# mLSTM head loop of a two-block kernel: a second buffer for the backward scores, and another order of work on four engines

## The reference

```python
def mlstm_scan(q, k, v, ig, log_fg):      # per chunk, with running maximum m_t
    log_d = cum[..., :, None] - cum[..., None, :] + igc[..., None, :]
    d_mat = jnp.exp(jnp.where(tril, log_d, -jnp.inf) - m_t[..., None])
    scores = jnp.einsum('bhtd,bhsd->bhts', qc, kc) * d_mat
    num = jnp.einsum('bhts,bhse->bhte', scores, vc) + ...
    den = jnp.sum(scores, axis=-1) + ...
    h_out = num / jnp.maximum(jnp.abs(den), jnp.exp(-m_t))[..., None]

h_m = (mlstm_scan(q_m, k_m, v_m, ig_fwd, lfg_fwd)
       + flip_seq(mlstm_scan(flip_seq(q_m), flip_seq(k_m), ...)))
mlstm_out = head_rmsnorm(from_heads(h_m), mlstm_g, MLSTM_HEADS) * jax.nn.sigmoid(m_o)
return jnp.concatenate([hgrn_out, mlstm_out], axis=-1) @ w_out
```

## Time and profile before

| | us |
|---|---|
| median of 3 runs | 1682.1 |
| lowest and highest | 1680.78, 1685.4 |
| the profiled execution | 1681.14 |
| its span in the trace | 1679.3 |
| mLSTM loop in it, from the first g to the first out2 product | 1047.61 to 1104.73 |

### The profile page before, as it was taken

How to read it: one execution, slowest core, us unless ns; L and a number is a source line. 1 busy time by engine, 2 the same in 40 slices (tenths; PEclk the granted TensorE clock), 3 DMA queues, 4 the chain that set the end, 5 groups by cost and what they waited for, 6 DMA issues and landing times.

```text
span 1679.3 us, 18987 instructions
## 1 busy us (share of the span) xinstructions
PE 1616.4 (96%) x7258; PEld 1270.9 (76%) x7258; DVE 981.5 (58%) x1412; ACT 686.3 (41%) x1066; POOL 148.4 (9%) x153
## 2 busy tenths in 40 slices
PE   5999999999999999999999999789999999999997
PEld 1588765677888888887888787578877888888885
DVE  6986687775644334546788596655434553535352
ACT  4521465324443123335554578836433322212131
POOL 0221000252000000013000000332000100000001
PEclk9999999999999999999999999899999999999999
DMA  9544114422232233223232021235111322222221
GB/s 312 191 150 141 60 52 151 151 101 93 60 100 88 93 121 100 81 76 119 98 135 92 26 70 57 94 117 209 50 51 51 113 88 101 100 100 100 100 100 50
DMA packets 112600, 173.89 MB, mean 104 GB/s; under 512 B 3851, under 2 KB 56651, under 8 KB 112012
## 3 DMA queue, kind: packets, MB, share of 16 engines
q1 hardware_dynamic: 108220, 158.05, 27.8%
q0 software_dynamic: 4304, 14.81, 2.7%
HBM read 168.53 MB, written 4.33 MB: 103 GB/s over the span
## 4 chain that ended last, share of the span: by engine, by line
PE 83%; DVE 9%; DMA 3%; ACT 2%; issue 2%; SPq 1%; DVEq 0%; ACTq 0%
PE bank L896 17%; PE bank L898 17%; PE bank L897 17%; PE bank L933 6%; PE bank L934 6%; PE bank L938 5%; DMA weight_slots<-in_w_mod 2%; PE bank L1206 2%; PE bank L1126 1%; PE bank L1138 1%; PE bank L1444 1%; PE bank L1336 1%; DVE weight_slots_lo L2377 1%; PE bank L1401 1%; PE bank L1426 1%
## 5 line engine op out<-in xcount | busy, mean ns | idle before, releaser
L3260 POOL TENSOR_TENSOR arena<-arena 128x512 f32<-128x512 f32 (+1 forms) x56 | 76.7, 1377 | 970.7 <-ACT arena L1651 966.9
L898 PE MATMUL bank<-hx_hi,weight_slots_lo 128*128 128x512 f32 x320 | 124.7, 390 | 0.0
L3215 DVE TENSOR_TENSOR weight_slots_lo<-weight_slots,weights_hi 128x2048 fp32r<-128x2048 f32 x30 | 67.4, 2289 | 95.5 <-ACT weights_hi L2336 95.5
L2336 ACT ACTIVATE weights_hi<-weight_slots 128x2048 fp32r<-128x2048 f32 x30 | 55.8, 1909 | 161.1 <-DMA weight_slots<-in_w_up 115.5
L1620 ACT ACTIVATE weights_hi<-weight_slots 128x2048 fp32r<-128x2048 f32 (+2 forms) x46 | 77.3, 1723 | 90.1 <-DMA weight_slots<-in_ffn_w_down 57.6
L897 PE MATMUL bank<-xn_lo,weights_hi 128*128 128x512 f32 x288 | 112.1, 389 | 0.0
L896 PE MATMUL bank<-sq_hi,weights_hi 128*128 128x512 f32 x256 | 99.6, 389 | 0.0
L897 PE MATMUL bank<-sq_lo,weights_hi 128*128 128x512 f32 x256 | 99.6, 389 | 0.0
L898 PE MATMUL bank<-sq_hi,weight_slots_lo 128*128 128x512 f32 x256 | 99.6, 389 | 0.0
L1606 ACT ACTIVATE arena<-bank 128x512 f32<-128x512 f32 (+2 forms) x99 | 49.1, 532 | 94.2 <-PE bank L898 45.6
L2377 DVE TENSOR_TENSOR weight_slots_lo<-weight_slots,weights_hi 128x2048 fp32r<-128x2048 f32 (+2 forms) x35 | 68.1, 1981 | 27.0 <-ACT weights_hi L1620 27.0
(11 more groups left out here) (459 smaller groups left out, 4077.6 us busy)
## 6 DMA issues: line engine op xcount, KB each, us to landing
weight_slots<-in_w_in SPq DMA_DIRECT2D x24, 1024.0 KB, 7.5
weight_slots<-in_ffn_w_up SPq DMA_DIRECT2D x22, 1024.0 KB, 6.4
weight_slots<-in_w_up SPq DMA_DIRECT2D x16, 1024.0 KB, 6.8
weight_slots<-in_w_down SPq DMA_DIRECT2D x16, 1024.0 KB, 6.8
weight_slots<-in_w_mod SPq DMA_DIRECT2D x14, 1024.0 KB, 10.3
arena<-in_w_mod POOLq DMA_DIRECT2D x32, 256.0 KB, 3.3
weight_slots<-in_w_out SPq DMA_DIRECT2D x8, 1024.0 KB, 7.8
weight_slots<-in_w_xkv SPq DMA_DIRECT2D x8, 1024.0 KB, 7.5
```

The source lines that it names most:

```text
L898: return mm(ps, ll, rh, start=False, stop=stop)
L2336: A(W_hi[:, s % 2, a:b], W[:, s % 2, a:b], ACT.Copy).then_inc(w_hi, 1)
L3215: V.tensor_tensor(W_lo[:, s % 2, a:b], W[:, s % 2, a:b], W_hi[:, s % 2, a:b].bitcast(F32), ALU.subtract).then_inc(w_lo, 1)
L3260: G.tensor_tensor(acc, acc, sq[i % 2][:, 0:width], ALU.add).then_inc(sq_added, 1)
```

## The change

All of it lies in and around the loop over the four heads.

- **Buffers.** The score tiles were one set for each direction (`S2`). Now the forward scores have one set, and the backward scores have two, used by even and odd heads. The new one is at tiles 66 to 69. `head_scores` of the backward direction waits for num_b of two heads before, no longer for that of the head before. Because the region of tiles 66 to 69 is written again by a later load of x, SP now also waits for num_2_b_1 before that load.
- **DVE.** The forward and the backward scores of head h + 1 run behind each other in cycle h. Before, the backward ones ran at the start of cycle h + 1. `head_scaled(h - 1)` comes behind them, `lstm_out(h - 1)` behind `directions_added(h)`. The split of half 1 of the out2 weights moves from cycle 3 to the end of cycle 2. The low parts of the hgrn tiles and of heads 0 to 2 move behind the loop.
- **ACT.** The decays of head 1, both directions, come directly before the loop. In cycle h both decays of head h + 2 run. Before, cycle h held the backward decay of h + 1 and the forward one of h + 2. The output gates with their two table loads move from ahead of the loop to cycle 1. The high parts of the hgrn tiles and of heads 0 and 1 move to the end of cycle 2. Both halves of the out2 weights are split in cycle 2 ahead of `head_factor(2)`.
- **PE.** The transposes of head h - 1 come behind num backward of head h, no longer ahead of it.

The number of instructions and their shapes stay as they are.

The core of the diff:

```diff
--- before.py
+++ after.py
@@ jobs
+        if h >= 0:
+            j += [f"num_{h}_b_{p}" for p in range(2)]
         if h >= 1:
             j += [f"ht_{h - 1}"]
-        if h >= 0:
-            j += [f"num_{h}_b_{p}" for p in range(2)]
@@ buffers
-        S2 = [tiles(32, 4), tiles(36, 4)]
+        S2_f, S2_b = tiles(32, 4), [tiles(66, 4), tiles(36, 4)]
+
+        def S2(h, d):
+
+            return S2_b[h % 2] if d else S2_f
@@ SP
+            done(sp, f"num_{HEADS - 2}_b_1")
             load(xb, x_rest, "x_back")
@@ PE (and S2(h, d) in state_output)
+                if h >= 0:
+                    state_output(h, 1)
                 if h >= 1:
                     head_transposed(h - 1)
-                if h >= 0:
-                    state_output(h, 1)
@@ ACT
             decay(1, 0, "f")
+            decay(1, 1, "b")
+
+            def output_gates():
+
+                for m in range(HC):
+                    evicted(act, f"mo_{m}")
+                    A(mix2[:, 4 + m, :], mix2[:, 4 + m, :], ACT.Sigmoid).then_inc(sem("gate_ready"), 1)
+                log_exp_tables()
...
             for h in range(HEADS):
                 forward_scaled(h)
-                if h + 1 < HEADS:
-                    decay(h + 1, 1, "b")
-                if h == 0:
+                if h == 1:
+                    output_gates()
+                if h + 2 < HEADS:
+                    decay(h + 2, 0, "f")
+                    decay(h + 2, 1, "b")
+                elif h + 2 == HEADS:
+                    split_w("out2", 0)
+                head_factor(h)
+                if h + 2 == HEADS:
                     act.wait_ge(sem("ho_gated"), HEADS)
                     for k in range(HC):
                         split_x(mix2_hi[:, k, :], mix2[:, k, :])
-                else:
-                    lstm_high(h - 1)
-                if h + 2 < HEADS:
-                    decay(h + 2, 0, "f")
-                elif h + 2 == HEADS:
-                    split_w("out2", 0, (0,))
-                head_factor(h)
-                if h + 2 == HEADS:
-                    split_w("out2", 0, (1,))
+                    lstm_high(0)
+                    lstm_high(1)
+            lstm_high(2)
             split_w("out2", 1)
             lstm_high(HEADS - 1)
@@ DVE
-                if h:
-                    done(dve, f"num_{h - 1}_{c}_1")
+                if h > d:
+                    done(dve, f"num_{h - 1 - d}_{c}_1")
...
-            head_scores(0, 0, "f")
+            for d, c in enumerate("fb"):
+                head_scores(0, d, c)
+            head_normed(3)
+            head_gated(3)
             for h in range(HEADS):
-                head_scores(h, 1, "b")
-                if h == 0:
-                    head_normed(3)
-                    head_gated(3)
-                else:
+                forward_limits(h)
+                if h + 1 < HEADS:
+                    for d, c in enumerate("fb"):
+                        head_scores(h + 1, d, c)
+                if h:
                     head_scaled(h - 1)
-                forward_limits(h)
-                if h + 1 == HEADS:
-                    split_w("out2", 0, (1,))
+                directions_added(h)
                 if h:
                     lstm_out(h - 1)
-                if h + 1 < HEADS:
-                    head_scores(h + 1, 0, "f")
-                directions_added(h)
-                if h == 0:
-                    for k in range(HC):
-                        split_x("mix2", k, mix2_lo[:, k, :], mix2[:, k, :], mix2_hi[:, k, :])
-                else:
-                    lstm_low(h - 1)
+                if h + 2 == HEADS:
+                    split_w("out2", 0, (1,))
+            for k in range(HC):
+                split_x("mix2", k, mix2_lo[:, k, :], mix2[:, k, :], mix2_hi[:, k, :])
+            for h in range(HEADS - 1):
+                lstm_low(h)
             head_scaled(HEADS - 1)
```

More of the change, by code:

```diff
@@ L1425, in state_output @@
                                 evicted(pe, f"g_{h}_{j}")
-                            ins = mm(out_, S2[d][:, j, P * i:P * i + P], Vm[:, j, h, :], start=j == sources[0], stop=j == sources[-1])
+                            ins = mm(out_, S2(h, d)[:, j, P * i:P * i + P], Vm[:, j, h, :], start=j == sources[0], stop=j == sources[-1])
                     end(ins)
@@ L2218, in _ @@
             norm_factor("norm_ho_3", features=P)
-            for m in range(HC):
-                evicted(act, f"mo_{m}")
-                A(mix2[:, 4 + m, :], mix2[:, 4 + m, :], ACT.Sigmoid).then_inc(sem("gate_ready"), 1)
-            log_exp_tables()
             decay(1, 0, "f")
+            decay(1, 1, "b")
[4 more added lines that the diff above has]
+                log_exp_tables()
             def lstm_high(h):
@@ L3037, in head_scores @@
                     g = full(dve, f"g_{h}_{j}")
[L3038 removed]
+                    ins = V.scalar_tensor_tensor(S2(h, d)[:, j, lo:hi], g[:, lo:hi], float(P) ** -0.5, mD(h, c)[n][:, lo:hi],
                                                  ALU.mult, ALU.mult)
```

1 line of the change is left out of this document (removed).

## The result

| us | before | changed |
|---|---|---|
| median (4 runs each on one chip) | 1682.77 | 1668.62 |
| lowest and highest | 1680.78, 1685.40 | 1666.98, 1669.01 |
| the profiled execution, and its span | 1681.14, 1679.3 | 1666.98, 1665.2 |
| loop: first g to first out2 product | 1047.61 to 1104.73 = 57.12 | 1047.07 to 1090.65 = 43.58 |
| first to fifth out2 product | 22.35 | 22.36 |

The ratio of the times is 0.9914, 95% interval 0.9901 to 0.9926. 14.15 us are gone from the median. In the profiled execution 13.54 of them are gone from the loop. The profiled execution of the changed kernel is the fastest of its four; its median lies 1.64 us above it. Behind T0 nothing was given back.

The account below looks back on a forecast made before the run. PE, busy 96%, could regain only waits (17.7 us for DVE's scores) and low-clock time; afterwards ACT's queue is longest. Loop gain 13.0 less 1.0 for clock gives 12.0: 1681.14 to 1669.1, plus 0.96 for median 1670.1; range 1665.5 to 1676.

Parts of the forecast that it names:

- T0: Start of the first out2 product, where the loop ends: 1104.73 before, forecast 1091.7, a gain of 13.0 us.
- the clock cost: Out2 starting at PE's lower clock after two waits: 0 to 2.0 us, taken as 1.0 against the gain.
- ACT's queue: ACT from 1051.7 to its first weight half: decays, scalings, gates, factors, half sum to 30.6 us without gaps, ending 1082.3.
- POOL and DVE block each other: Out2 weight halves: DVE's, ready near 1084.2, waits for POOL's until 1086.9, then takes 2.27, ending 1089.1.
- the banks: At out2's start: banks of num forward of head 3 were claimed not to be among the first four; no size given.
- no blocking: Rival: POOL and DVE weight halves do not block; head 3's forward scaling sets T0 near 1090.2; 1668.6, chance 0.08.
- the second set of tiles: Backward score tiles: with both directions in one run, a second set can take away PE's 17.7 us of waits.
- the change does not do what it says: Rival: PE waited for ACT, not the single buffer; moving the gates alone gives all; forecast's time, no separate chance.
- Table loads at twice their row: Rival: the gates' two loads on ACT each take 1.3 us more, 2.6 in all; 1672.7, chance 0.05.
- Handoffs of 0.15 us: Rival: some twenty ACT and DVE links take 0.15 us more each, T0 3 to 4 later; 1674, chance 0.11.
- rivals of the low clock: PE at 1.2 GHz through the loop (no gain, 1681) or on through out2 (slower, 1691.4); chance 0.04 each.
- the slower rival: Low clock stays through out2: the 22.35 us behind T0 take 44.7; 1691.4, chance 0.04.

Follow-up runs that it names:

- e11: Changed kernel with the four hgrn splits back in cycle 0 on ACT and DVE; median 1672.06, loop 45.70 us.
- e12: Changed kernel with two more ACT table loads among the output gates in cycle 1, same numbers computed; median 1674.24, loop 46.31 us.
- e6: Changed kernel with DVE's out2 weight half moved to cycle 3, behind the scaling of head 2; median 1668.94, loop 42.76 us.
- e10: e8 with ACT's first weight half moved to cycle 1 and most hgrn splits behind forward scaling of head 3; median 1672.15, loop 45.25 us.
- e9: Changed kernel with the decays back in the cycles they had before the change; median 1682.49, loop 56.00 us.
- e1: Changed kernel with one set of backward score tiles instead of two; median 1669.27, loop 43.59 us.
- e3: Changed kernel with the output gates ahead of the loop and one set of backward score tiles; median 1675.83, loop 47.51 us.
- e2: Changed kernel with the output gates and their table loads ahead of the loop again; median 1670.00, loop 42.80 us.
- e7: Changed kernel with the transposes of the previous head ahead of num backward again; median 1672.82, loop 47.03 us.
- e8: Changed kernel with both edits of e2 and e6: gates ahead of the loop, DVE's weight half later; median 1670.32, loop 41.57 us.
- e5: Kernel before the change with only the output gates moved to cycle 1; median 1680.89, loop 56.07 us.

## Why the prediction held, step by step

The forecast was 1670.1 and the median came to 1668.62; a profiled 1669.1 stood against 1666.98. Of these 2.1 us, 0.54 lies ahead of the loop, 1.0 is the clock cost, and 0.5 is in the loop. That the median is nearer, by 1.5 us, is luck: the forecast put it 0.96 above the profiled execution, and it lay 1.64 above. Times below are compared after taking 0.54 off the forecast's.

| step | forecast | minus 0.54 | trace |
|---|---|---|---|
| first decay | 1051.7 | 1051.2 | 1051.23 |
| ACT's first half done, POOL half begins | 1082.4 | 1081.9 | 1082.00 |
| POOL half ends | 1086.9 | 1086.4 | 1086.53 |
| DVE half ends | 1089.1 | 1088.6 | 1088.68 |
| head 2 scaled | 1090.8 | 1090.3 | 1090.18 |
| T0 | 1091.7 | 1091.2 | 1090.65 |

- **ACT's queue** was the right model. The sum of 30.6 us from rows of before was good to 0.3 us, and the claim of no gaps held. e11 and e12 confirm it from outside: 2.14 us of splits gave 2.12, 2.71 us of loads gave 2.73.
- **POOL and DVE block each other:** the forecast had 4.9 us for the DVE half, the trace 4.94. e6 shows 2.28 without POOL beside it. "SBUF — State Buffer" of the Trainium skill, "SBUF: two separate sides", calls the port pair that the two engines share an exclusive lock, held for the whole instruction by whichever starts first; among DVE's instructions it names those with two inputs in SBUF. The traces agree, with 4.94 here, 4.47 in e10, where POOL was 0.62 us ahead, and 0.74 for the instruction that reads a bank. In e9 `head_scaled(1)` began 0.82 us ahead of POOL's half, behind POOL's transfer issue, and was held all the same.
- **The end of the loop:** 0.9 us were set aside for the transposes and handoffs. They took 0.47 (1090.18 to 1090.65). This is the 0.5 us within the loop.
- **The clock cost** of 1.0 was mis-sized. The step allowed for the two waits before T0 to leave PE at the low clock when out2 begins, and took the middle. They did not: the granted clock was back at 1.00 at 1086 us, and the wait of 2.56 behind it did not lower it. From T0 to the fifth product it was 22.36 us, against 22.35. The range taken, 0 to 2.0, was nearly right all the same: e1, e3, e12 paid 1.6, e2 paid 1.1, e7 0.5, and e8 2.5. The reason given for the middle, that both waits are shorter than the 5.5 and 7.1 behind which the level was low, misses a row that it had: behind the wait of 4.16, shorter than 4.9, the 14 records take 2.45, 0.18 each, and the granted clock in the kernel before was 0.50 from 1083 to 1085.
- **PE's waits:** forecast 4.9, 3.5 and little else, 9 in all. Measured 4.87, 2.56 and 0.41, 7.8 in all. The second is shorter because head 3's products ended at 1087.67, where the forecast less 0.54 has 1086.9; they ran longer at the low clock than it had.
- **A wrong step: the banks.** The prediction said that the banks of num forward of head 3 are not among the first four of out2. They are. In e6 and e8 the first out2 product waits 1.49 and 2.02 us for ACT L2204. In the changed kernel that scaling ended at 1090.40, 0.25 us before T0, so the mistake cost nothing. One of the prediction's rivals, no blocking, had this dependence right, with a T0 1.5 us earlier; e6, which takes the blocking away, gained 0.8.
- **A wrong attribution: the second set of tiles.** The prediction gave the 17.7 us of waits to the second set and the one run of both directions together. e1 shows the same loop without the set. The gain belongs to the order: both directions' scores in one run need the decays a cycle sooner (e9: without them, nothing is gained), late hgrn splits (5.4 us alone in the old order, 2.1 in the new), and late transposes (3.45). The second set and the gates' place stand in for each other (e1, e2, e3). No run puts the scores of the two directions apart again with all else as changed, so the share of that edit alone is not shown. That before the change PE waited for the bank and not for the tile, as the prediction itself said, fits e1; with the gates first one set is not enough (e3).
- **The rivals.** Moving the gates alone gives 1 us of loop (e5), so "the change does not do what it says" falls. Table loads at twice their row fall with e12. Handoffs of 0.15 us fall with the table above. Both rivals of the low clock asked for it through the loop or through out2; in the changed kernel it holds for one stretch, which begins during the wait ahead of the transposes at 1080.30 and is over by 1086. The price of the slower rival rested on the 22.35 us behind T0, where the worst that a run showed was 2.5 more (e8).
- **The load of x and the low parts behind the loop** cost nothing: from the fifth product to the end of the span it is 552.2 us in both kernels.

**No version beat the changed kernel in the median.** e6 and e8 shorten the loop by 0.8 and 2.0 us. Their medians are 1668.94 and 1670.32, with intervals that overlap. The profiled executions show where the gains went. That of e6 begins its loop 0.77 us later than that of the changed kernel and takes 1.8 more behind the fifth out2 product. That of e8 begins 1.64 later and takes 2.5 more to the fifth product and 1.7 behind it. One of the four executions of e8 took 1666.53, at a mean granted clock of 0.995 (the other three 1670.12 to 1670.89, at 0.991 and 0.992). That is below all four of the changed kernel, but it was not profiled.

## What to carry to other kernels

When one buffer makes an engine wait, add up the whole queue of each other engine from the last common event: here one sum of start-to-start times on ACT gave the end of its part to 0.3 us, and with the steps behind it the loop to 0.5 us. The second buffer did not matter in this order, and was worth 4.7 us in another. Edits can be substitutes; only runs with each of them and with both undone tell. Before moving a long elementwise POOL instruction, look at what DVE starts within its 4.5 us, since an instruction of 0.7 us on the critical path, with its inputs in SBUF, that arrives second pays what is left of it.

## What the runs showed of the hardware that was not expected

**The same loss of clock can fall on work that is waited for, or on work that is not.** In the changed kernel the granted clock falls during the wait of 4.87. The low level then lies on the products of head 3, and PE waits 2.56 us behind them anyway, so it costs nothing. The clock is back by 1086 and stays at 1.00 through that wait and T0. In e8 the waits of PE between 1070 and 1086 are 1.01 and 0.42, and the clock is 1.00 up to 1088. It falls only then, within the wait of 2.02 ahead of T0, and the low level lies on the first out2 products, which pay 2.5 us (columns as in the earlier trace rows):

```profile
1088.00:1089.00 1.00, 0.26 (x3) 0.02 (x1) 1.00 (x1) 1.00 (x3) 0.00 (x0) 0.94 1.02 430
...
1091.00:1092.00 1.00, 1.00 (x4) 0.81 (x3) 0.93 (x5) 0.00 (x0) 0.00 (x0) 0.50 0.07 16
```

Why 2.56 us of waiting did not lower the clock in one kernel, and 1.26 and 2.02 did in the other, stays open. Far behind the loop there is a second such place. From 1260 to 1280 us, first the changed kernel, then e6:

```profile
1260.00:1280.00 20.00, 18.36 (x76) 13.28 (x75) 10.55 (x17) 6.27 (x13) 0.00 (x0) 1.00 0.00 1
```

```profile
1260.00:1280.00 20.00, 18.36 (x69) 13.15 (x68) 10.53 (x17) 6.24 (x13) 0.00 (x0) 0.91 0.00 1
```

PE is busy 18.36 us in both, but the clock is 0.91 in e6, as in e3, e8, e10 and e12, and 1.00 in the changed kernel, e1, e2, e7 and e11. From the fifth out2 product to the end of the span it is 554.0 us in e6 and 552.2 in the changed kernel: 1.8 us for a stretch in which the two run the same instructions. What decides it stays open; only one execution of each kernel was profiled. For comparisons of this kernel's orders it means that a loop shorter by up to 2 us need not show in the time: e8's did not in three of its four executions.

**Table loads** in the middle of a full ACT queue cost 1.29 us each from start to start, with nothing behind them. **DVE against POOL:** an instruction of DVE whose inputs are both in SBUF and that begins beside POOL's weight half is held until POOL is done, and 0.62 us was enough to make 0.68 into 4.47 (e10). The short ones (0.68 alone) end 0.54 to 0.56 us behind POOL's half, in the kernel before and in e5, e6, e8, e9 and e10; DVE's weight half (2.27 alone) ends 2.14 to 2.16 behind it, in the changed kernel and in e1, e2, e11 and e12. Scores, which read a bank, are not held: four of them take 1.69 us beside POOL's half in e3 (from 1084.93), as they do elsewhere.
